# One convolution tap more on the ScalarE and GpSimd route, one fewer on VectorE

## The reference

```python
def causal_dwconv(u, prev, w, bias):
    ext = jnp.concatenate([prev.astype(u.dtype), u], axis=1)
    y = lax.conv_general_dilated(ext, w[:, None, :].astype(u.dtype), window_strides=(1,), padding='VALID',
                                 dimension_numbers=('NWC', 'WIO', 'NWC'), feature_group_count=u.shape[-1])
    return y + bias, ext[:, -(w.shape[0] - 1):]

def conformer_conv(x, prev, w_in, b_in, w_dw, b_dw, g_n, b_n, w_out, b_out):
    a, gate = jnp.split(x @ w_in + b_in, 2, axis=-1)
    u = a * jax.nn.sigmoid(gate)
    u, new_prev = causal_dwconv(u, prev, w_dw, b_dw)
    u = jax.nn.silu(layer_norm(u, g_n, b_n))
    return u @ w_out + b_out, new_prev
```

## Time and profile before

| | |
|---|---|
| median of 3 runs | 2707.59 us (2704.77 to 2711.15) |
| the profiled execution | 2711.12 us, its span 2709.3 us |
| mean granted TensorE clock in it | 0.978 |
| PE busy | 2606.3 us, 96% of the span |
| DVE busy | 1553.8 us, 57% |
| ACT busy | 1179.5 us, 44% |
| POOL busy | 247.0 us, 9% |

### The profile page before, as it was taken

How to read it: one execution, slowest core, us unless ns; L and a number is a source line. 1 busy time by engine, 2 the same in 40 slices (tenths; PEclk the granted TensorE clock), 3 DMA queues, 4 the chain that set the end, 5 groups by cost and what they waited for, 6 DMA issues and landing times.

```text
span 2709.3 us, 48804 instructions
## 1 busy us (share of the span) xinstructions
PE 2606.3 (96%) x17562; PEld 2558.3 (94%) x17562; DVE 1553.8 (57%) x2295; ACT 1179.5 (44%) x1973; POOL 247.0 (9%) x218
## 2 busy tenths in 40 slices
PE   8999699999999999999979989999999999999996
PEld 7898699999999999999979869999999999999996
DVE  7999867744433454444567746686444334445555
ACT  7777644534332343343354534454343223433332
POOL 4888200000000000000010000000000000000001
PEclk9999799999999999999989969999999999999998
DMA  7544244444544444454443213444445434444542
GB/s 271 139 133 132 68 152 137 142 149 146 164 158 143 136 144 154 145 176 157 137 135 108 96 46 109 142 139 153 143 153 172 149 128 145 150 153 145 175 150 73
DMA packets 115065, 382.42 MB, mean 141 GB/s; under 512 B 29472, under 2 KB 29856, under 8 KB 114720
## 3 DMA queue, kind: packets, MB, share of 16 engines
q1 hardware_dynamic: 95328, 373.20, 41.9%
q0 software_dynamic: 992, 6.25, 0.7%
q10 hardware_dynamic: 18688, 2.21, 0.6%
HBM read 375.32 MB, written 8.27 MB: 142 GB/s over the span
## 4 chain that ended last, share of the span: by engine, by line
PE 84%; POOL 7%; DVE 4%; issue 2%; ACT 2%; POOLq 0%; DMA 0%; ACTq 0%; SPq 0%; DVEq 0%
PE acc L385 26%; PE acc L387 26%; PE acc L386 26%; POOL prods L321 7%; DVE w_lo L1063 1%; PE acc L411 1%; PE acc L412 1%; PE acc L413 1%; ACT prods L845 0%; PE ot L686 0%; PE ot L688 0%; PE pt L585 0%; ACT w_hi L706 0%; DVE xr L1158 0%; PE pt L508 0%
## 5 line engine op out<-in xcount | busy, mean ns | idle before, releaser
L385 PE MATMUL acc<-xh,w_hi 128*128 128x320 f32 x3584 | 1114.1, 311 | 17.1 <-DVE w_lo L1063 14.1
L386 PE MATMUL acc<-xl,w_hi 128*128 128x320 f32 x3584 | 1108.1, 309 | 0.0
L387 PE MATMUL acc<-xh,w_lo 128*128 128x320 f32 x3584 | 1108.1, 309 | 0.0
L706 ACT CAST w_hi<-w_raw 128x1024 fp32r<-128x1024 f32 (+1 forms) x648 | 698.5, 1116 | 535.6 <-PE acc L387 509.2
L1063 DVE TENSOR_TENSOR w_lo<-w_raw,w_hi 128x1024 fp32r<-128x1024 f32 (+1 forms) x648 | 839.4, 1335 | 156.1 <-ACT w_hi L706 156.1
L385 PEld LDWEIGHTS acc<-xh,w_hi 128*128 128x128 f32 x3584 | 673.3, 188 | 31.5 <-DVE w_lo L1063 20.4
L386 PEld LDWEIGHTS acc<-xl,w_hi 128*128 128x128 f32 x3584 | 673.4, 188 | 0.5
L387 PEld LDWEIGHTS acc<-xh,w_lo 128*128 128x128 f32 x3584 | 673.4, 188 | 0.0
L385 PE MATMUL acc<-h_split,w_hi 128*128 128x320 f32 x1408 | 435.4, 309 | 0.0
L386 PE MATMUL acc<-h_split,w_hi 128*128 128x320 f32 x1408 | 434.4, 309 | 0.0
L387 PE MATMUL acc<-h_split,w_lo 128*128 128x320 f32 x1408 | 434.4, 309 | 0.0
(11 more groups left out here) (210 smaller groups left out, 1984.0 us busy)
## 6 DMA issues: line engine op xcount, KB each, us to landing
w_raw<-in_up SPq DMA_DIRECT2D x352, 512.0 KB, 4.0
w_raw<-in_down SPq DMA_DIRECT2D x128, 704.0 KB, 4.7
w_raw<-in_w_in SPq DMA_DIRECT2D x64, 512.0 KB, 6.1
w_raw<-in_w_out SPq DMA_DIRECT2D x32, 512.0 KB, 4.0
w_raw<-in_w_q SPq DMA_DIRECT2D x32, 512.0 KB, 4.2
w_raw<-in_w_o SPq DMA_DIRECT2D x32, 512.0 KB, 4.1
w_raw<-in_w_kv SPq DMA_DIRECT2D x8, 512.0 KB, 4.0
out_y<-xr SPq DMA_DIRECT2D x4, 640.0 KB, 3.0
```

What stands on the lines that cost most here:

```text
L385: pe.matmul(out, wh, hi[:, k, 0:width], start=first, stop=False)
L386: pe.matmul(out, wh, lo[:, k, 0:width], start=False, stop=False)
L387: mm = pe.matmul(out, wl, hi[:, k, 0:width], start=False, stop=last)
L706: act.copy(w_hi[:, slot, 0:n], w_raw[:, slot, 0:n]).then_inc(hi_ready, 1)
```

## The change

One constant changes, and with it the second one that is derived from it:

```diff
 VECTOR_CENTERS = 3
-POOL_TAPS = 13
+POOL_TAPS = 14
 DVE_TAPS = CW - POOL_TAPS
```

## The result

The change makes the kernel slower: 2719.93 us, median of 5 runs (2719.24 to 2720.59), against 2707.52 us (2704.77 to 2711.15). The ratio is 1.0047, 95% interval 1.0036 to 1.0058, or 12.4 us more. The profiled execution took 2720.28 us with a span of 2718.5.

The account below looks back on a forecast made before the run. GpSimd's additions were taken to bound the first 294 us. Terms for tiles 0 to 15 summed to 11.9 to 16.9 us; 14.8 was added to the median 2707.59 us, giving 2722.4 us, range 2714 to 2730.

Parts of the forecast that it names:

- GpSimd becomes the bound in every tile: First 294 us: GpSimd's additions run back to back and alone set a tile's time, as idle time is at most 0.62 us.
- VectorE's tap is worth nothing: VectorE's taps: one fewer saves 0.46 us a tile, but the wait at the join takes it up.
- dearer form: Blocking by w_lo chunks: one addition blocked 2.88 us, two of 1.69; tiles 2 to 13 each 1.05 us longer.
- ScalarE's product is hidden: ScalarE before u_seg: the extra 0.48 us product fits in 1.39 us of idle time.
- The price of the addition: GpSimd, tiles 2 to 13: a fourteenth free addition of 1.02 us makes each tile 0.70 or 1.05 us longer.
- milder form: Blocking by w_lo chunks: four additions of about 1.7 us; tiles 2 to 13 each 0.70 us longer.
- The phase of 8.98 us: Tiles of the first 294 us: the first w_lo chunk starts 8.98 us after the tile's first addition.
- Tile 15: TensorE's sum at the phase's end: 14 products in place of 13, two matmul records more, 0.5 us.
- A: First 294 us, faster: VectorE sets the pace and the addition hides; gain 6.9 us, 2700.7 us; chance 4%.
- B: First 294 us, no visible change: tap gain and addition meet halfway by better w_lo phase, under 5.4 us; chance 5%.
- C: First 294 us, smaller loss: blocked time per tile pair unchanged, idle time all used; 8.3 us, 2715.9 us; chance 11%.
- D: First 294 us, larger loss: both chunk pairs block an addition 2.88 us every tile; 22.7 us, 2730.3 us; chance 8%.

Follow-up runs that it names:

- e1: Kernel before with tap 30 left out, so VectorE runs 17 taps and GpSimd still adds 13: 2708.15 us, ratio 0.9996.
- e2: Changed kernel with VectorE keeping its 18 taps (tap 17 computed twice), 14 products and 14 additions: 2723.42 us, ratio 1.0048.
- e3: Kernel before with one more product on ScalarE that nobody adds, 14 products and 13 additions: 2701.47 us, ratio 0.9968.
- e7: Kernel before, same work, only the semaphore counting products goes up by 14 a tile in place of 13: 2701.91 us, ratio 0.9980.
- e4: Changed kernel, but in phase w_in VectorE makes only the first half of each w_lo chunk: 2694.39 us, ratio 0.9939.
- e6: Changed kernel with GpSimd's 14 additions in two interleaved chains, added at the end: 2699.58 us, ratio 0.9970.
- e11: Changed kernel with an 80-column memset on VectorE between taps and w_lo chunks from tile 2 on: 2721.74 us, ratio 1.0057.

## Why the prediction was right

**GpSimd becomes the bound in every tile.** Right, by the vanished idle time, the 1.93 us wait at every join, and e1, in which GpSimd bound every tile with 13 additions once VectorE had one tap less. ScalarE waits 2.9 to 3.9 us before u_seg in the five tiles looked at, where it had waited 1.39 us in the tighter of two tiles before: longer, as foretold.

**VectorE's tap is worth nothing.** Nearly: 0.06 us a tile in e1. In e2 it was worth 0.29 us on average, by five tiles of the dearer form.

**ScalarE's product is hidden.** Right. In e3 a product more did no harm, and e7, without it, showed the same tile (16.16 and 16.13 us).

**The price of the addition.** 1.02 us, less the idle time of 0.62, plus 0.30 for the fourth chunk, which in the even tiles had met idle time: 0.70 in the milder form, 0.73 measured. That the blocked time can't shrink stood on four chunks that each meet an addition of a GpSimd that is never idle. The profile after has the four blocked additions, and e4 shows the blocked time to come from the chunks.

**The knife's edge.** The range 11.9 to 16.9 us held at its lower end, with 12.4 between the medians. In the two profiles the phase itself grew by 11.7 us, just under that end, so part of the hit is scatter between runs. My point, 2722.4, was 2.5 us too high, because I weighed the dearer form by how often the odd tiles had shown it, four to two, while the changed kernel shows none in twelve. The phase of 8.98 us, predicted from the rows of before, came out to the hundredth. The prediction rightly said that it leaves both forms open. What it did not look at is the running addition: it took each addition to stand where it stood in the tile, and the ninth moved by 0.08 us. The table above shows that in most kernels this sorts the forms. So that the milder form came in all twelve tiles was foreseen by nothing in the sum.

**The other terms.** Tile 0 1.05 (1.0 to 1.4), tile 1 1.03 (1.0), tile 14 1.07 (1.0 to 1.4). Tile 15 was mis-sized: 0.5 us more was predicted. From the join of tile 14 to that of tile 15 it is 12.6 us after and 12.9 before, 0.3 less. Where the granted clock rises within the sum was worth more than the two records, and the prediction kept that place fixed.

**The rivals.** A needed an addition under 0.6 us, and one costs 1.02. B needed fewer than three or four blocked additions, and there are four. C, the smaller loss, needed the fourth chunk to meet idle time still; it didn't. D's tile of 18.1 us did come in length, though not in the changed kernel and not in D's way: five tiles of e2 took 18.2 us, with one addition blocked for 3.2 us and two for 1.7, where D had two of 2.88. The granted clock that D mentioned did fall more often: it is 0.90 in three of tiles 2 to 13 (3, 5 and 12) and was so in one before. These three tiles take 17.36 to 17.39 us and are none the longer for it.

## What to carry to other kernels

Before you move work to an engine with a low busy share, cut the stage at its loop and read the idle time there: GpSimd was busy 9% of the span and had 0.62 us a tile to spare, less than the 1.02 us of one addition. Price a step by its distance to the next one and not by its length: of 1.02 us an addition took 0.88, the rest was its wait for its predecessor. Two interleaved chains took that away and gained more than any split of the taps did. And where two engines block each other, count the collision on both sides: the fewer additions GpSimd had, the shorter was the mean tile, down to 12, even with VectorE as the bound. With the chains the steps are small (16.02, 15.95, 15.79 us), and the intervals of neighbouring runs overlap.

## What the runs showed of the hardware that was not expected

- The hand-over between two dependent GpSimd additions is 0.14 us when a semaphore wait and a register operation stand between them (step 1.02, before), and 0.08 us when one instruction does (step 0.96, e3 and e7). For additions that don't wait for each other the step is 0.84 us (e6), less than the 0.88 us that one lasts.
- An addition that meets two w_lo chunks of some 1.2 us is either blocked over both (2.9, up to 3.2 us) or let in between them (1.7 us, the second chunk then takes 1.9). Both happened in one kernel with the chunk at the same place in the tile within 0.03 us. Where a tap precedes the chunk, the dearer form came when the chunk started less than 0.10 us before an addition's end or up to 0.12 us after the next one's start (before, e1, e2, e3, e7). With a memset before the chunk (e11) it did not come at 0.03 to 0.07 us. The full condition is open.
- With two interleaved chains a blocked addition is recorded as 1.86 us long, since it starts 0.18 us earlier behind the one before (e6; steps of 0.84 and 1.02 us).
